# Softmax probabilities scaled by GpSimd instead of VectorE, in a two-layer hybrid attention and convolution block

## The reference, cut to what matters

```python
def _attend(q, k, v):
    s = jnp.einsum('bqkgd,bskd->bkgqs', q, k).astype(jnp.float32) * (HEAD_DIM ** -0.5)
    p = jax.nn.softmax(s, axis=-1).astype(v.dtype)
    return jnp.einsum('bkgqs,bskd->bqkgd', p, v)
```

```python
    br_a = (o_attn * jax.nn.silu(z_a)) @ w_pa
    ...
    merged = jax.nn.sigmoid(g_a) * br_a + jax.nn.sigmoid(g_b) * br_b + jax.nn.sigmoid(g_c) * br_c
    return merged @ w_o
```

## Time and profile before

| what | us |
|---|---|
| median of 3 runs (2678.72 to 2680.15) | 2679.32 |
| the profiled execution | 2684.73 |
| its span in the trace | 2682.9 |
| TensorE busy | 2622.7 (98%) |
| VectorE busy | 1726.5 (64%) |
| ScalarE busy | 845.5 (32%) |
| GpSimd busy | 1003.1 (37%) |
| from 140 to 700 (layer 0's attention): TensorE, VectorE, GpSimd busy | 557.95, 319.63, 107.08 of 560 |
| from 1612 to 2060 (layer 1's attention): TensorE, VectorE, GpSimd busy | 447.20, 292.91, 103.19 of 448 |

### The profile page before, as it was taken

One profiled execution on the slowest core, in us unless ns is written; L12 is line 12 of the kernel. 1 busy time (PEld: TensorE's weight loads), 2 busy tenths in 40 slices (PEclk: granted clock), 3 DMA queues, 4 the chain that ended last, 5 costly groups with the idle time before them and its releaser, 6 DMA issues.

```text
span 2682.9 us, 32363 instructions
## 1 busy us (share of the span) xinstructions
PE 2622.7 (98%) x13218; PEld 2157.5 (80%) x13218; DVE 1726.5 (64%) x1788; ACT 845.5 (32%) x1220; POOL 1003.1 (37%) x883
## 2 busy tenths in 40 slices
PE   7999999999999999999999999999999999999997
PEld 4888888888887888888878778888888888887875
DVE  3756566655129988846657765777773399866755
ACT  3234444444200000034314433555552000006324
POOL 3632121211243333334575763212124455554550
PEclk8999999999999999999999999999999999999998
DMA  6011111111264011124333512110112211114432
GB/s 270 32 65 50 40 50 40 50 44 50 83 212 186 32 40 40 36 89 157 129 121 138 180 40 75 36 44 36 40 49 78 79 48 48 47 59 139 140 110 86
DMA packets 74595, 220.48 MB, mean 82 GB/s; under 512 B 8400, under 2 KB 11728, under 8 KB 73424
## 3 DMA queue, kind: packets, MB, share of 16 engines
q1 hardware_dynamic: 51984, 178.03, 19.4%
q10 hardware_dynamic: 22464, 40.38, 4.0%
HBM read 173.29 MB, written 45.09 MB: 81 GB/s over the span
## 4 chain that ended last, share of the span: by engine, by line
PE 90%; DVE 6%; ACT 1%; issue 1%; DMA 1%; POOL 0%; SPq 0%; ACTq 0%; DVEq 0%; POOLq 0%
PE PS L768 50%; PE PS L920 21%; PE PS L956 6%; PE PS L978 6%; PE PS L965 5%; DVE cv L1731 1%; DMA wmA<-wmod 1%; PE PS L829 1%; PE PS L942 1%; DVE e L1795 1%; PE PS L823 1%; DVE e L1804 1%; DVE kd L1598 0%; PE PS L844 0%; PE PS L1117 0%
## 5 line engine op out<-in xcount | busy, mean ns | idle before, releaser
L656 POOL CAST wh<-wraw 128x512 fp32r<-128x512 f32 (+1 forms) x394 | 321.7, 817 | 1211.6 <-PE PS L768 587.6
L658 POOL TENSOR_TENSOR wl<-wraw,wh 128x512 fp32r<-128x512 f32 (+1 forms) x394 | 570.4, 1448 | 31.5
L1731 DVE SCALAR_TENSOR_TENSOR cv<-hc,vec,cv 128x1024 f32<-128x1024 f32 x360 | 435.7, 1237 | 8.8
L768 PE MATMUL PS<-Uh,wh 128*128 128x512 f32 (+1 forms) x1536 | 429.1, 375 | 7.4 <-ACT Uh L1146 5.8
L768 PE MATMUL PS<-Uh,wl 128*128 128x512 f32 (+1 forms) x1536 | 422.6, 371 | 0.0
L768 PE MATMUL PS<-Ul,wh 128*128 128x512 f32 (+1 forms) x1536 | 421.2, 370 | 0.0
L1697 DVE TENSOR_TENSOR PTl<-PS,PTh 128x512 fp32r<-128x512 f32 x328 | 226.8, 691 | 280.0 <-ACT PTh L1261 279.4
L920 PE MATMUL PS<-Uh,wh 128*128 128x512 f32 (+1 forms) x960 | 358.0, 373 | 2.2 <-POOL wl L658 2.2
L920 PE MATMUL PS<-Uh,wl 128*128 128x512 f32 (+1 forms) x960 | 357.4, 372 | 0.0
L920 PE MATMUL PS<-Ul,wh 128*128 128x512 f32 (+1 forms) x960 | 357.2, 372 | 0.0
L1261 ACT ACTIVATE PTh<-PS 128x512 fp32r<-128x512 f32 x328 | 196.2, 598 | 447.7 <-PE PS L965 447.0
(11 more groups left out here) (164 smaller groups left out, 3538.7 us busy)
## 6 DMA issues: line engine op xcount, KB each, us to landing
wraw<-w SPq DMA_DIRECT2D x156, 512.0 KB, 3.4
graw<-stg ACTq DMA_DIRECT2D x88, 256.0 KB, 2.0
wmB<-wmod SPq DMA_DIRECT2D x32, 512.0 KB, 7.0
e<-graw SPq DMA_DIRECT2D x24, 640.0 KB, 4.0
wraw<-w SPq DMA_DIRECT2D x48, 256.0 KB, 4.1
e<-graw SPq DMA_DIRECT2D x24, 512.0 KB, 3.6
wmA<-wmod SPq DMA_DIRECT2D x8, 1024.0 KB, 12.1
hL<-hT_in SPq DMA_DIRECT2D x8, 640.0 KB, 22.0
```

Of the source, the lines that this page charges most:

```text
L656: nc.gpsimd.tensor_copy(hi[:, s], wraw[par][:, s]).then_inc(whi[par], 1)
L658: nc.gpsimd.tensor_tensor(lo[:, s], wraw[par][:, s], hi[:, s].bitcast(F32), ALU.subtract).then_inc(wsplit[par], 1)
L768: ins = mmul(PS[:, at + c:at + c + m], w[:, k * P:(k + 1) * P], x[:, k, c0 + c:c0 + c + m], start=(first and a == 0), stop=(last and a == 2))
L1731: ins = stt(cv[:, i, c0:c0 + n], hc[:, i, CPAD * who + c0 + tap:CPAD * who + c0 + tap + n], vec[:, l, wt:wt + 1], cv[:, i, c0:c0 + n], ALU ...
```

## The change

`norm` exists on two engines now. VectorE still waits for the exponentials and makes the inverse of the sums, at the same places of its queue, and raises a new semaphore `s_ri`. GpSimd waits for `s_ri`, multiplies the probabilities by the inverse in place, and raises `s_pn`, for which TensorE waits as before. On GpSimd the product stands, in the steps that `norms_at` names, behind the `dup` of the step and ahead of its `refill`; in a layer's start it stands behind the `refill` of the same slice.

```diff
@@ gpsimd
+                def norm(un, h):
+
+                    p = Pr[:, un % 2, h, :units[un][3] * P]
+                    pool.wait_ge(s_ri, 4 * (ub + un) + h + 1)
+                    nc.gpsimd.tensor_scalar(p, p, ri[:, un % 2, h:h + 1], None, ALU.mult).then_inc(s_pn, 1)
+
...
                 for i in range(4):
                     refill(("p", i))
+                    norm(0, i)
                 dup(3)
                 for un, kt in steps_of(l):
                     if kt == q_at(units[un][3]) and un + 4 < len(units):
                         dup(un + 4)
+                    if un + 1 < len(units):
+                        for h in norms_at(units[un][3], kt):
+                            norm(un + 1, h)
                     refill((un, kt))
@@ vector, norm(un, h)
-                    x, nk = 4 * (ub + un) + h, units[un][3]
-                    p, r = Pr[:, un % 2, h, :nk * P], ri[:, un % 2, h:h + 1]
+                    x = 4 * (ub + un) + h
                     dve.wait_ge(s_exp, x + 1)
                     if x >= 8:
                         dve.wait_ge(s_pn, x - 7)
-                    st.done(nc.vector.reciprocal(r, rs[:, un % 2, h:h + 1]))
-                    ts(p, p, r, None, ALU.mult).then_inc(s_pn, 1)
+                    nc.vector.reciprocal(ri[:, un % 2, h:h + 1], rs[:, un % 2, h:h + 1]).then_inc(s_ri, 1)
```

More of the change, by code:

```diff
@@ L476, in build @@
         s_pv = sem("pv_done")
+        s_ri = sem("inverse_sum")
         s_pn = sem("probs_normalised")
```

## The result

The changed kernel takes 2811.63 us (2811.0 to 2812.46) against 2679.74 us for the kernel before on the same chip: a ratio of 1.0485, with a 95% interval of 1.0473 to 1.0498 (the two medians alone give 1.0492). The profiled execution took 2811.0 us, its span is 2809.2, and that is 126.3 us more than the span of before. The difference is smaller than the 132 us of the medians because the profiled execution of before lay 5.4 us over its median. Slower was forecast, but by 18 us.

The account below looks back on a forecast made before the run. TensorE was taken to bound the kernel, so the change could only cost: 5.5 + 2.4 + 6.9 + 3.4 = 18.2 us on 2679.3 gave 2697.5 us, 0.7% slower. The range for 8 in 10 was 2690 to 2716.

Parts of the forecast that it names:

- What bounds the kernel: TensorE, busy for 98% of the span; in both attention stretches it waits 2.7 us, never for the scaled probabilities.
- the removal at 0: Taking 144 multiplications, 127.2 us, off VectorE gives TensorE nothing earlier; costed at 0.
- The length of a split: GpSimd's split in attention, without VectorE multiplications beside it, has its undisturbed length of 3.85 us.
- The price D: One GpSimd multiplication of 1,280 columns, taken as 1.3 us, near the cast, with ends of 1.24 and 2.95.
- The formulas of the queue: TensorE's lateness from GpSimd's order of products and splits, in terms of D; waits of 14.8 us in all.
- start of layer 1: First unit of layer 1's attention: head 3's product stands behind a split, so TensorE starts 5.5 us late.
- start of layer 0: First unit of layer 0's attention: head 3's product stands behind a split, so TensorE starts 2.4 us late.
- layer 1, units 8, 9, 14, 15: They follow units with a split in step 7, between two products: 1.7 us late each, four times, 6.9 us.
- Units that cost nothing: Ordinary units: GpSimd has 2.5 us in layer 1, 3.9 in layer 0, before the next unit; cost 0.
- The second rival: GpSimd's product costs 2.95 us, as on two tiles; each layer 1 unit late, about 2745 us or more; chance 0.10.
- The clock: TensorE's granted clock drops behind each of the two starts, 1.7 us each, 3.4 us; nothing for waits of 1.7 us.
- the first rival: GpSimd's product is dearer, about 2.1 us: 33 us with the clock, 2712 us; chance 0.18.

Follow-up runs that it names:

- Experiment 8: The changed kernel with the product left out on both engines; VectorE makes the inverse and frees TensorE at once: 2683.5 us, ratio 1.0003 to the kernel before.
- experiment 1: The changed kernel with a GpSimd copy of the 1,280 probabilities onto themselves in place of the product, scaling left out: ratio 1.0053 to the kernel before.

## Why the prediction was wrong, point by point

**What bounds the kernel, and the removal at 0.** Right. Experiment 8 measured the removal at 0.0003 of the time, with 0.9993 to 1.0012. TensorE had no wait that VectorE's load made.

**The length of a split.** Right: 3.83 us from 1703.80 to 1707.63 at layer 1's start, and no cast beside a product of VectorE any more.

**The price D.** This is the step that failed. I took 1.3 us, "near the cast, since the inverse is one number a row and not a second stream", and the trace has 3.52 us. The operands said nothing about the price: a copy and a product by a constant have the same one tile in and one out, and take 1.26 and 3.45 us; the product with a repeated second input takes 2.32, and the one with a number a row 3.52. Worse, the 2.95 us of an operation on two full tiles stood as the far end, and the real price lies beyond it. An operation that the trace does not show was held between two rows of other operations, and neither row bounded it. The estimate of 1.92 us, worked out from the best case that the Trainium skill names (GPSIMD Engine Reference, section 3.1), was nearer and also too low; here the measurement decides.

**The formulas of the queue.** Right at the price for which they were made, as experiment 1 showed at 1.26 us, and at most of their places at 3.52 us too. With D = 3.52:

| place | formula | with 3.52 | measured |
|---|---|---|---|
| start of layer 1 | 4.2 + D | 7.7 | 7.58 |
| start of layer 0 | 1.1 + D | 4.6 | 6.53 |
| layer 1, units 8, 9, 14, 15 | 2D - 0.88 | 6.2 | 5.99, 5.97, 5.99, 5.98 |
| layer 0, units 1, 2, 11, 12 | 2D - 3.0 | 4.0 | 3.87, 3.92, 3.87, 3.87 |
| layer 1, units 1, 2, 3, 10 to 13 | 2D - 4.73 | 2.3 | 2.15 to 2.17, seven times |

Of these, only the start of layer 0 is off, since at this price the product of head 2 still runs when the split could begin; the formula had the split begin on time. The other measured numbers lie 0.1 to 0.2 us under the formulas. Units 4 to 7 of layer 1 are ordinary units too, with a split in step 3 or 5 of the unit before, and they waited longer, 3.40 to 4.82 us: at this price a split there pushes the last product as well, which no formula of the prediction held. The same happened at units 3, 4, 13 and 14 of layer 0, with 2.0 us each, and three of the short units waited 2.0 us together. Summed over all their places, ordinary units included, the formulas give 78 of the 95 us of waits.

**Units that cost nothing.** The prediction gave the point from which ordinary units of layer 1 turn late, a D of 2.4, and the price lay beyond it. The second rival was therefore the right case, with the right mechanism ("two products end 5.9 us after the inverse of head 2, the unit begins 4.8 after it"), at a still higher price: 64 us of waits at 2.95, 94 at 3.52. It had a chance of 0.10 and was left out of the range, and even its 2745 us lie 67 under what was measured. Two of the prediction's own signs of being wrong came true: a product of over 1.8 us, and waits at ordinary units.

**The clock.** The mechanism was right, the size was not. 3.4 us were set for two drops of 1.7; 31.6 us were lost, in 16 drops of 1.4 to 3.0. In experiment 1, with the two drops that the prediction had, the clock cost 4.3 us. In the changed kernel a drop came with each of the twelve waits of 3.8 us and more, and with only four of the thirteen between 2.0 and 3.5: of seven waits of 2.15 to 2.17 us one had a drop behind it. So the two idle times of the earlier trace rows could not say what a wait of 2 or 3 us would cost. The drops make the price enter twice.

**The range.** Its upper end, 2716, let the first rival in and shut the second out. With D open between 1.24 and 2.95, each us of D was worth 10 us of waits near the price taken (two starts at D, four units at 2D), 18 from 1.5 on, and some 40 from 2.4 on, so the sum was steep on one side. The range should have followed the steep side.

## What to carry to other kernels

An engine with spare time is no place for work that is due: what counts is the distance from the moment at which the input is ready to the moment at which the result is waited for, and what stands in the queue between. Write the lateness as a formula of the unknown price, find the price at which the covered cases turn late, and if that point lies within the possible prices, let the range reach beyond it. And when only an operation of another kind has a row, treat it as a guess and not as a bound.

## What the runs showed of the hardware

- GpSimd, float32, 128 x 1,280 elements in place: copy 1.26 us, product with a second input repeated along the row 2.32, product by a constant 3.45, product by one number a row 3.52. From 256 to 1,280 columns the last grows from 0.92 to 3.52, 2.5 ns a column; the copy by 0.8 and the one with a repeated input (0.61 to 2.32) by 1.7. The product that reads a second input for every element is cheaper than the two that do not.
- An operation of GpSimd on two tiles took 2.95 us at 1,280 columns, with VectorE idle beside it, and the product whose second input is one repeated column 2.32.
- TensorE did 834 matmuls more and finished 30 us earlier, because it was not idle: with 16 of the 25 waits of 2.0 to 7.6 us the granted clock fell to 0.5, and stood there for some us behind them; with the waits filled it stayed at 1.00.
- GpSimd's products of 640 columns stretched from 1.88 to 2.24 us where VectorE multiplied for 0.55 us at the same moment. Those of 1,280 columns kept their 3.52 us beside VectorE's other work in attention.
